# Gated mixer's core: products with the values as three products of upper and lower parts

## The chip, the cores and the metric

The kernel runs on one core of a Trainium2 chip. The time is that of one execution on the device in microseconds (us), the median of three runs of the kernel before. TensorE, VectorE (DVE in rows), ScalarE (ACT), GpSimd (POOL) and SyncE (SP, which starts the transfers of the weights) each run their own list of instructions in order and meet by semaphores.

## What is computed

A decoder trunk of two layers over 512 tokens of width 1024, in float32. Each layer is a feed-forward part, a mixer, a cross attention to 256 memory tokens and a second feed-forward part. The mixer of the second layer is a gated linear attention, the only part that is touched here:

```python
def gla_mixer(h, w_in, w_g2, b_g, head_norm, w_out):
    q, k, v, g_lr, r = _split(h @ w_in, ODD_SPLITS)
    gk = jax.nn.log_sigmoid((g_lr @ w_g2 + b_g).astype(jnp.float32)) / GLA_TAU
    ...
    q_dec = q * jnp.exp(G)
    k_inv = k * jnp.exp(-G)
    k_rem = k * jnp.exp(G_last - G)
    att = jnp.where(tril, jnp.einsum('bnhid,bnhjd->bnhij', q_dec, k_inv), 0.0)
    o_intra = jnp.einsum('bnhij,bnhjv->bnhiv', att, v)

    def step(state, xs):
        qd, kr, vv, dec = xs
        o = jnp.einsum('bhid,bhdv->bhiv', qd, state)
        state = dec[..., None] * state + jnp.einsum('bhjd,bhjv->bhdv', kr, vv)
        return state, o
    ...
    o = rmsnorm(o, head_norm).reshape(Bb, S, GLA_DV).astype(h.dtype) * jax.nn.silu(r)
    return o @ w_out
```

It has 4 heads of 128 query and key and 256 value columns, and chunks of 64 tokens.

## The kernel before

The program is one function, `trunk`, with a list of work for each engine, written out by hand in order; `parts` lists the eight parts, and the gated mixer is part 5, with a function `gla` on every engine. Weights come as units of 512 KB. SyncE loads a unit into `w_raw`, ScalarE rounds it to its upper part (`split_hi`, L412), and VectorE subtracts that from the unit, which leaves the lower part (`split_lo`, L417). `split_units(i, seg, n, off)` does this for `n` units, four units ahead of the one that TensorE reads. Large products are then made of three products of the type float32r: upper by upper, and the two mixed ones (`three`, L479 to L481; `values`, L2178 to L2180). A product of two plain float32 tiles is one matmul call, which the trace shows as two loads of the stationary operand (PEld) and two MATMUL records.

In `gla` the projections run in the order q, k, v, r, out. The values v of 4 x 128 tokens by 1024 columns are made in two halves, in the banks 4 to 7 and then 0 to 3 of PSUM, and ScalarE copies each half to `g_v` with one instruction over four banks (L1236 and L1239, semaphore `v_ready`). TensorE then transposes `g_kr` (k_rem) in four times four blocks (L2526, banks 4 to 7), ScalarE copies them to `g_krt` (L1243), and TensorE projects seven of the eight units of r (`project`, L479 to L481, banks 0 and 1), which ScalarE copies through Silu (L970) with a split behind each copy. Before its loop ScalarE loads the table for Sqrt (L1247).

The core is a loop over sixteen steps w, four heads n for each of four tiles T of 128 tokens. TensorE does in step w:

- scores (L2560): `g_k` by `g_q`, 128x128, plain float32, into a bank that two steps share; waits for the mask of step w-2
- states (L2566): for the two chunks a of the tile, 64 rows of `g_krt` by 64 rows of `g_v`, 128x256, each into a bank of its own; the two use the upper and lower 64 rows of the array; waits for S of step w-2
- `mixed(w - 1)`: scores times values (L2543, `g_att` by `g_v`, 128x256), which waits for the mask and for both states of step w-1; then the query times the state (L2549, 64 output rows for each chunk) on top of it in the same bank

VectorE does in step w: the mask (L1922, PSUM to `g_att`), then the states of the two chunks (L1931 a copy, where there is none before, L1933 otherwise; in the last tile only one). In step 0 it also splits one unit (L417). Behind steps 7, 11 and 15 it takes the norm of a tile that is done (`mean` L1954 and L1955, `normed` L1963 and four times L1966). ScalarE copies `mixed` to `f` (L1251) and squares it (L1254, semaphore `osq`), and every fourth step takes a root (L1258). `w_free`, `p_free`, `att_full`, `att`, `S`, `o_full` are semaphores.

## Time and profile before

| | us |
|---|---|
| median of 3 runs | 2206.42 (2205.71 to 2206.72) |
| the profiled execution | 2203.32 |
| its span on the core | 2201.6 |
| TensorE busy in the span | 2181.0 |
| VectorE busy | 1458.9 |
| ScalarE busy | 1125.9 |

The profiled execution is one of its own; its time is 3.1 us under the median. The span is the stretch from the first to the last instruction. A busy TensorE counts the records of its matmuls, whose ends are modelled: consecutive records overlap, so what a group of matmuls costs is read from the chain, where each piece ends as the next begins.

### The profile page before, as it was taken

How to read it: one execution, taken by the hardware profiler on the slowest of the kernel's cores; microseconds unless marked ns; L12 is line 12 of the kernel's file. 1: busy time of each engine (PE TensorE's matmuls, PEld its weight loads, DVE VectorE, ACT ScalarE, POOL GpSimd, SP SyncE). 2: the span in 40 equal slices, each digit the busy share in tenths (PEclk: the TensorE clock that was granted, in tenths of full speed). 3: DMA queues.
4: the chain of work that ended last, by engine and by line, in shares of the span. 5: the costliest groups of instructions: out<-in, count | busy, mean ns of one | idle time of the engine just before them, and what ended most of it. 6: DMA issues, size and time to landing. Idle time of an engine off the chain costs nothing.

```text
span 2201.6 us, 36639 instructions
## 1 busy us (share of the span) xinstructions
PE 2181.0 (99%) x13844; PEld 1943.8 (88%) x13844; DVE 1458.9 (66%) x2187; ACT 1125.9 (51%) x1881; POOL 108.6 (5%) x102
## 2 busy tenths in 40 slices
PE   9999999999999999999999999999999999999999
PEld 8999888765888899998899998887858888999987
DVE  7888535797666598874388885345266666888732
ACT  6555534467554555563265554245345546555531
POOL 0000000575000000000000000000000000000000
PEclk9999999999999999999999999999999999999999
DMA  4333332221352233333323333322304422333332
GB/s 162 107 104 96 115 104 74 77 86 39 125 172 67 77 115 105 105 109 101 115 87 105 103 97 115 108 88 82 100 27 145 154 77 77 105 105 105 108 100 79
DMA packets 61953, 221.44 MB, mean 101 GB/s; under 512 B 7953, under 2 KB 8081, under 8 KB 61858
## 3 DMA queue, kind: packets, MB, share of 16 engines
q1 hardware_dynamic: 57456, 208.69, 29.0%
q10 hardware_dynamic: 4402, 11.46, 1.5%
q8 instruction: 62, 1.02, 0.2%
q14 instruction: 33, 0.27, 0.0%
HBM read 218.03 MB, written 2.10 MB: 100 GB/s over the span
## 4 chain that ended last, share of the span: by engine, by line
PE 91%; DVE 6%; ACT 1%; issue 1%; DMA 0%; POOL 0%; DVEq 0%; SPq 0%; POOLq 0%; ACTq 0%
PE ps L2082 12%; PE ps L2084 12%; PE ps L2083 12%; PE ps L2178 11%; PE ps L2180 11%; PE ps L2179 11%; PE ps L479 6%; PE ps L480 5%; PE ps L481 5%; PE ps L2018 1%; DVE e_sc L1746 1%; DVE e_max L1745 1%; DVE w_lo L417 1%; DVE e_sc L1761 1%; PE ps L2566 0%
## 5 line engine op out<-in xcount | busy, mean ns | idle before, releaser
L417 DVE TENSOR_TENSOR w_lo<-w_raw,w_hi 128x1024 fp32r<-128x1024 f32 x206 | 256.7, 1249 | 362.2 <-ACT w_hi L412 361.3
L412 ACT ACTIVATE w_hi<-w_raw 128x1024 fp32r<-128x1024 f32 x210 | 221.6, 1057 | 319.7 <-PE ps L2180 224.5
L2082 PE MATMUL ps<-t_hi,w_hi 128*128 128x256 f32 x1280 | 362.3, 283 | 1.1 <-ACT tmp L843 1.1
L2083 PE MATMUL ps<-t_lo,w_hi 128*128 128x256 f32 x1280 | 362.2, 283 | 0.0
L2084 PE MATMUL ps<-t_hi,w_lo 128*128 128x256 f32 x1280 | 362.2, 283 | 0.0
L2082 PE MATMUL ps<-x_hi,w_hi 128*128 128x256 f32 x960 | 271.7, 283 | 0.0
L2083 PE MATMUL ps<-x_lo,w_hi 128*128 128x256 f32 x960 | 271.7, 283 | 0.0
L2084 PE MATMUL ps<-x_hi,w_lo 128*128 128x256 f32 x960 | 271.7, 283 | 0.0
L1475 DVE TENSOR_TENSOR w_lo<-f,w_hi 128x1024 fp32r<-128x1024 f32 x152 | 186.2, 1225 | 123.0 <-ACT w_hi L830 123.0
L479 PE MATMUL ps<-x_hi,w_hi 128*128 128x256 f32 (+1 forms) x736 | 250.9, 341 | 0.5 <-ACT g_v L1239 0.2
L2082 PEld LDWEIGHTS ps<-t_hi,w_hi 128*128 128x128 f32 x1280 | 245.7, 192 | 1.3 <-ACT tmp L843 1.3
L480 PE MATMUL ps<-x_lo,w_hi 128*128 128x256 f32 (+1 forms) x736 | 246.0, 334 | 0.0
L2084 PEld LDWEIGHTS ps<-t_hi,w_lo 128*128 128x128 f32 x1280 | 245.8, 192 | 0.0
L2083 PEld LDWEIGHTS ps<-t_lo,w_hi 128*128 128x128 f32 x1280 | 245.7, 192 | 0.0
L481 PE MATMUL ps<-x_hi,w_lo 128*128 128x256 f32 (+1 forms) x736 | 245.7, 334 | 0.0
L2178 PE MATMUL ps<-w_hi,act_hi 128*128 128x512 f32 x608 | 236.6, 389 | 0.0
L2179 PE MATMUL ps<-w_lo,act_hi 128*128 128x512 f32 x608 | 236.6, 389 | 0.0
L2180 PE MATMUL ps<-w_hi,act_lo 128*128 128x512 f32 x608 | 236.5, 389 | 0.0
L843 ACT ACTIVATE tmp<-ps 128x256 f32<-128x256 f32 x320 | 123.1, 385 | 173.9 <-PE ps L2084 171.1
L830 ACT ACTIVATE w_hi<-f 128x1024 fp32r<-128x1024 f32 x152 | 160.4, 1055 | 86.2 <-PE ps L2084 84.1
L2082 PEld LDWEIGHTS ps<-x_hi,w_hi 128*128 128x128 f32 x960 | 184.3, 192 | 0.0
L2083 PEld LDWEIGHTS ps<-x_lo,w_hi 128*128 128x128 f32 x960 | 184.3, 192 | 0.0
(350 smaller groups left out, 4311.9 us busy)
## 6 DMA issues: line engine op xcount, KB each, us to landing
w_raw<-in_wstream SPq DMA_DIRECT2D x310, 512.0 KB, 3.3
w_raw_odd<-in_wstream SPq DMA_DIRECT2D x80, 512.0 KB, 3.4
tmp<-in_post_gains ACTq DMA_DIRECT2D x8, 512.0 KB, 4.9
gain_bc<-in_gains ACTq DMA_DIRECT2D x7, 512.0 KB, 3.8
h<-in_x SPq DMA_DIRECT2D x4, 512.0 KB, 6.0
c_mem<-in_mem ACTq DMA_DIRECT2D x2, 1024.0 KB, 4.9
out_dram<-h SPq DMA_DIRECT2D x3, 512.0 KB, 2.7
c_gain<-in_mem_gains ACTq DMA_DIRECT2D x2, 512.0 KB, 6.4
```

What stands on the lines that cost most here:

```text
L412: nc.scalar.activation(weights(v)[0], raw(v), ACT.Copy).then_inc(w_hi_ready, 1)
L417: nc.vector.tensor_tensor(wl, raw(v), wh.bitcast(f32), ALU.subtract).then_inc(w_ready, 1)
L479: nc.tensor.matmul(dst, wh, xh, start=start, stop=False)
L480: nc.tensor.matmul(dst, wh, xl, start=False, stop=False)
L481: return nc.tensor.matmul(dst, wl, xh, start=False, stop=stop)
L1475: nc.vector.tensor_tensor(wl, S[:, n * UW:(n + 1) * UW], wh.bitcast(f32), ALU.subtract)\
L2082: nc.tensor.matmul(dst, wh[:, at], xh[:, b, :], start=first, stop=False, skip_group_check=True)
L2083: nc.tensor.matmul(dst, wh[:, at], xl[:, b, :], start=False, stop=False, skip_group_check=True)
L2084: last = nc.tensor.matmul(dst, wl[:, at], xh[:, b, :], start=False, stop=final, skip_group_check=True)
L2178: nc.tensor.matmul(dst, ah, wh, start=start, stop=False)
L2179: nc.tensor.matmul(dst, ah, wl, start=False, stop=False)
L2180: return nc.tensor.matmul(dst, al, wh, start=False, stop=stop)
```

## The change

`g_v`, `g_krt` and `g_att` are each replaced by an upper and a lower part of type float32r, and the state products and the scores times values are made of three products. ScalarE writes the upper parts and VectorE the lower ones:

- v: ScalarE copies two banks at a time (`g_v_hi`, four instructions in place of two), and VectorE subtracts for each pair (`v_lower`, four instructions). `v_ready` counts 1 behind the first half's two pairs, and 2 and 3 behind the pairs of the second half. TensorE starts the projection of r at 2, and the core at 3.
- krt: ScalarE copies as before, into `g_krt_hi`, and VectorE subtracts (four instructions). `g_krt` now has the order head, tile.
- scores: ScalarE copies the masked scores (`att_upper`), for step w+1 ahead of its work on step w, and for step 0 ahead of the loop; VectorE subtracts behind the states of the step, and `mixed` waits for that (`att_ready`).
- `g_v_lo` lies where `f` lies, `g_krt_lo` where `g_kr` lies. The scores and the query times the state stay plain float32.

```diff
@@ -87,6 +87,8 @@
         with ExitStack() as early:
             c_v_lo = early.enter_context(nc.sbuf_tensor("c_v_lo", [P, MT, DM], f32r))
             c_p_lo = early.enter_context(nc.sbuf_tensor("c_p_lo", [P, 2, MT, SEQ], f32r))
+        with ExitStack() as early:
+            g_v_lo = early.enter_context(nc.sbuf_tensor("g_v_lo", [P, TT, DM], f32r))
         f = sb("f", [P, TT, DM])
 
         x_hi = sb("x_hi", [P, KT, SEQ], f32r)
@@ -173,10 +175,15 @@
                 return own.enter_context(nc.sbuf_tensor(name, shape, dt))
             g_q = part_sb("g_q", [P, GH, SEQ])
             g_k = part_sb("g_k", [P, GH, SEQ])
+            with ExitStack() as early:
+                g_krt_lo = early.enter_context(nc.sbuf_tensor("g_krt_lo", [P, GH, TT, P], f32r))
             g_kr = part_sb("g_kr", [P, GH, SEQ])
-            g_krt = part_sb("g_krt", [P, TT, GH, P])
-            g_v = part_sb("g_v", [P, TT, DM])
+            g_krt_hi = part_sb("g_krt_hi", [P, GH, TT, P], f32r)
+            g_v_hi = part_sb("g_v_hi", [P, TT, DM], f32r)
             g_r = part_sb("g_r", [P, KT, SEQ])
+            with ExitStack() as early:
+                g_att_hi = early.enter_context(nc.sbuf_tensor("g_att_hi", [P, 2, P], f32r))
+                g_att_lo = early.enter_context(nc.sbuf_tensor("g_att_lo", [P, 2, P], f32r))
             g_lr = part_sb("g_lr", [GR, SEQ])
             g_w2 = part_sb("g_w2", [GR, GH * GDK])
             g_t = part_sb("g_t", [P, 2, SEQ])
@@ -395,7 +402,7 @@
 
             return b == 2 and i > 0 and parts[i - 1][0] == "cross"
 
-        VG = {"ffn": 0, "cross": 2, "even": 1, "gla": 2}
+        VG = {"ffn": 0, "cross": 2, "even": 1, "gla": 3}
         V0 = [sum(VG[k] for k, _, _ in parts[:i]) for i in range(NP)]
 
         ATI = {"ffn": 0, "cross": XH * TT, "even": AH * TT, "gla": 0}
@@ -1233,20 +1240,31 @@
                     if n + 1 < GH:
                         gate_log(n + 1)
                 act.wait_ge(w_free, U[i, "v"] + 6)
-                nc.scalar.activation(g_v[:, :, 0:SEQ], ps[:, 4:8, :], ACT.Copy).then_inc(v_ready, 1)
+                for b in range(0, TT, 2):
+                    nc.scalar.activation(g_v_hi[:, b:b + 2, 0:SEQ], ps[:, 4 + b:6 + b, :], ACT.Copy).then_inc(gs["v_hi"], 1)
                 split_units(i, "v", 3, GH)
                 act.wait_ge(w_free, U[i, "v"] + 10)
-                nc.scalar.activation(g_v[:, :, SEQ:2 * SEQ], ps[:, 0:4, :], ACT.Copy).then_inc(v_ready, 1)
+                for b in range(0, TT, 2):
+                    nc.scalar.activation(g_v_hi[:, b:b + 2, SEQ:2 * SEQ], ps[:, b:b + 2, :], ACT.Copy)\
+                        .then_inc(gs["v_hi"], 1)
                 split_units(i, "v", 1, KT - 1)
                 for n in range(GH):
                     act.wait_ge(gs["krT"], n + 1)
-                    nc.scalar.activation(g_krt[:, :, n, :], bank(4 + n).rearrange("p (t c) -> p t c", t=TT), ACT.Copy)\
-                        .then_inc(gs["krt"], 1)
+                    nc.scalar.activation(g_krt_hi[:, n, :, :], bank(4 + n).rearrange("p (t c) -> p t c", t=TT), ACT.Copy)\
+                        .then_inc(gs["krt_hi"], 1)
                 act.preload_act_table(ACT.Silu)
                 project(i, "r", KT - 1, g_r, func=ACT.Silu)
                 act.preload_act_table(ACT.Sqrt)
+
+                def att_upper(w):
+                    act.wait_ge(gs["att"], w + 1)
+                    nc.scalar.activation(g_att_hi[:, w % 2, :], g_att[:, w % 2, :], ACT.Copy).then_inc(gs["att_hi"], 1)
+
+                att_upper(0)
                 for w in range(TT * GH):
                     T, n = w // GH, w % GH
+                    if w + 1 < TT * GH:
+                        att_upper(w + 1)
                     act.wait_ge(gs["o_full"], w + 1)
                     nc.scalar.activation(f[:, T, n * GDV:(n + 1) * GDV], bank(4 + w % 2)[:, 0:GDV], ACT.Copy)
                     if w > 0:
@@ -1909,7 +1927,22 @@
                     nc.vector.tensor_tensor(g_k[:, n, :], g_k[:, n, :], g_t[:, 1, :], ALU.mult).then_inc(gs["qk"], 1)
                     if n + 1 < GH:
                         gate_sums(n + 1)
-                split_units(i, "v", GH, GH)
+                def v_lower(n):
+                    b, at = 2 * (n % 2), slice(n // 2 * SEQ, (n // 2 + 1) * SEQ)
+                    dve.wait_ge(gs["v_hi"], n + 1)
+                    return nc.vector.tensor_tensor(g_v_lo[:, b:b + 2, at], ps[:, 4 - 4 * (n // 2) + b:6 - 4 * (n // 2) + b, :],
+                                                   g_v_hi[:, b:b + 2, at].bitcast(f32), ALU.subtract)
+
+                v_lower(0)
+                v_lower(1).then_inc(v_ready, 1)
+                split_units(i, "v", 3, GH)
+                v_lower(2).then_inc(v_ready, 1)
+                v_lower(3).then_inc(v_ready, 1)
+                split_units(i, "v", 1, KT - 1)
+                for n in range(GH):
+                    dve.wait_ge(gs["krt_hi"], n + 1)
+                    nc.vector.tensor_tensor(g_krt_lo[:, n, :, :], bank(4 + n).rearrange("p (t c) -> p t c", t=TT),
+                                            g_krt_hi[:, n, :, :].bitcast(f32), ALU.subtract).then_inc(gs["krt"], 1)
                 project(i, "r", KT - 2)
                 dve.wait_ge(gs["qk"], 3 * GH)
                 dve.wait_ge(gs["zero"], 1)
@@ -1933,6 +1966,9 @@
                             ins = nc.vector.scalar_tensor_tensor(new, g_S[:, n, c % 3, :], g_dec[:, n, c:c + 1], up,
                                                                  ALU.mult, ALU.add)
                         link(ins) if a == 0 and c != SEQ // CH - 2 else ins.then_inc(gs["S"], 1)
+                    dve.wait_ge(gs["att_hi"], w + 1)
+                    nc.vector.tensor_tensor(g_att_lo[:, w % 2, :], g_att[:, w % 2, :], g_att_hi[:, w % 2, :].bitcast(f32),
+                                            ALU.subtract).then_inc(gs["att_ready"], 1)
                     if w == 0:
                         split_units(i, "r", 1, KT - 2)
                     if w % GH == GH - 1 and T > 0:
@@ -2529,19 +2565,22 @@
                 pe.wait_ge(v_ready, V0[i] + 2)
                 project(i, "r", KT - 1, x_hi, x_lo)
                 pe.wait_ge(gs["krt"], GH)
+                pe.wait_ge(v_ready, V0[i] + 3)
                 pe.wait_ge(p_free, PT0[i, "r"] + KT)
                 pe.wait_ge(gs["qk"], 3 * GH)
 
                 def mixed(w):
 
                     T, n = w // GH, w % GH
-                    pe.wait_ge(gs["att"], w + 1)
+                    pe.wait_ge(gs["att_ready"], w + 1)
                     pe.wait_ge(gs["S"], w + 1)
                     if w >= 2:
                         pe.wait_ge(gs["osq"], w - 1)
                     dst = bank(4 + w % 2)
-                    nc.tensor.matmul(dst[:, 0:GDV], g_att[:, w % 2, :], g_v[:, T, n * GDV:(n + 1) * GDV],
-                                     start=True, stop=False, skip_group_check=True)
+                    heads = slice(n * GDV, (n + 1) * GDV)
+                    for k, (a, v) in enumerate(((g_att_hi, g_v_hi), (g_att_hi, g_v_lo), (g_att_lo, g_v_hi))):
+                        nc.tensor.matmul(dst[:, 0:GDV], a[:, w % 2, :], v[:, T, heads], start=k == 0, stop=False,
+                                         skip_group_check=True)
                     for a in range(2):
                         c = 2 * T + a
                         if c == 0:
@@ -2561,10 +2600,11 @@
                                          start=True, stop=True).then_inc(gs["att_full"], 1)
                         if w >= 2:
                             pe.wait_ge(gs["S"], w - 1)
-                        for a in range(2):
-                            rows = slice(a * CH, (a + 1) * CH)
-                            last = nc.tensor.matmul(bank(2 + 4 * a + w % 2)[:, 0:GDV], g_krt[rows, T, n, :],
-                                                    g_v[rows, T, n * GDV:(n + 1) * GDV], start=True, stop=True)
+                        for m, (k, v) in enumerate(((g_krt_hi, g_v_hi), (g_krt_hi, g_v_lo), (g_krt_lo, g_v_hi))):
+                            for a in range(2):
+                                rows = slice(a * CH, (a + 1) * CH)
+                                last = nc.tensor.matmul(bank(2 + 4 * a + w % 2)[:, 0:GDV], k[rows, n, T, :],
+                                                        v[rows, T, n * GDV:(n + 1) * GDV], start=m == 0, stop=m == 2)
                         last.then_inc(gs["u_full"], 1)
                     if w >= 1:
                         mixed(w - 1)
```

TensorE, the first two steps of the core, before:

```order
L2560 MATMUL ps<-g_q,g_k 128x128
L2566 MATMUL ps<-g_v,g_krt 128x256 x2
L2560 MATMUL ps<-g_q,g_k 128x128
L2566 MATMUL ps<-g_v,g_krt 128x256 x2
L2543 MATMUL ps<-g_v,g_att 128x256
L2549 MATMUL ps<-g_S,g_q 64x256
```

And now:

```order
L2599 MATMUL ps<-g_q,g_k 128x128
L2606 MATMUL ps<-g_v_hi,g_krt_hi 128x256 x2
L2606 MATMUL ps<-g_v_lo,g_krt_hi 128x256 x2
L2606 MATMUL ps<-g_v_hi,g_krt_lo 128x256 x2
L2599 MATMUL ps<-g_q,g_k 128x128
L2606 MATMUL ps<-g_v_hi,g_krt_hi 128x256 x2
L2606 MATMUL ps<-g_v_lo,g_krt_hi 128x256 x2
L2606 MATMUL ps<-g_v_hi,g_krt_lo 128x256 x2
L2582 MATMUL ps<-g_v_hi,g_att_hi 128x256
L2582 MATMUL ps<-g_v_lo,g_att_hi 128x256
L2582 MATMUL ps<-g_v_hi,g_att_lo 128x256
L2588 MATMUL ps<-g_S,g_q 64x256
```

The groups stand in the same order; a state group is now three pairs of matmuls, and scores times values three matmuls. L2549 is now L2588.

VectorE, from the last unit splits before the core to the mask of step 1, before:

```order
L417 TENSOR_TENSOR w_lo<-w_raw,w_hi 128x1024 x10
L1922 COPY_PREDICATED g_att<-g_mask,ps 128x128
L1931 COPY g_S<-ps 128x256
L1933 SCALAR_TENSOR_TENSOR g_S<-g_S,g_dec,ps 128x256
L417 TENSOR_TENSOR w_lo<-w_raw,w_hi 128x1024
L1922 COPY_PREDICATED g_att<-g_mask,ps 128x128
```

And now:

```order
L1933 TENSOR_TENSOR g_v_lo<-ps,g_v_hi 128x2x512 x2
L424 TENSOR_TENSOR w_lo<-w_raw,w_hi 128x1024 x3
L1933 TENSOR_TENSOR g_v_lo<-ps,g_v_hi 128x2x512 x2
L424 TENSOR_TENSOR w_lo<-w_raw,w_hi 128x1024
L1944 TENSOR_TENSOR g_krt_lo<-ps,g_krt_hi 128x512 x4
L424 TENSOR_TENSOR w_lo<-w_raw,w_hi 128x1024 x6
L1955 COPY_PREDICATED g_att<-g_mask,ps 128x128
L1964 COPY g_S<-ps 128x256
L1966 SCALAR_TENSOR_TENSOR g_S<-g_S,g_dec,ps 128x256
L1970 TENSOR_TENSOR g_att_lo<-g_att,g_att_hi 128x128
L424 TENSOR_TENSOR w_lo<-w_raw,w_hi 128x1024
L1955 COPY_PREDICATED g_att<-g_mask,ps 128x128
```

The ten splits now have the lower parts of v and krt among them, and the lower part of the scores stands between the states and the unit split of step 0.

ScalarE, from the last split before the core into step 1, now; before, L1251 and L1254 (now L1269 and L1272) came right behind the table load:

```order
L419 ACTIVATE w_hi<-w_raw 128x1024
L1257 ACT_TABLE_LOAD
L1261 ACTIVATE g_att_hi<-g_att 128x128 x2
L1269 ACTIVATE f<-ps 128x256
L1272 ACTIVATE tmp,g_st<-ps 128x256
L1261 ACTIVATE g_att_hi<-g_att 128x128
L1269 ACTIVATE f<-ps 128x256
```

The upper part of the scores of steps 0 and 1 stands between the table load and the first copy.

## Rows read from the trace of the kernel before

**Rows 1.** The page: shares of the chain that ended last, by engine.

```profile
PE 91%; DVE 6%; ACT 1%; issue 1%; DMA 0%; POOL 0%; DVEq 0%; SPq 0%; POOLq 0%; ACTq 0%
```

**Rows 2.** Window: length, PE, PEld, DVE, ACT, POOL busy (x instructions); PEclk, DMA share, GB/s.

```profile
1556.00:1594.80 38.80, 38.58 (x173) 31.77 (x171) 8.59 (x7) 13.96 (x19) 0.00 (x0) 1.00 0.29 92
1594.80:1631.00 36.20, 36.12 (x186) 17.36 (x184) 24.37 (x66) 14.96 (x51) 0.00 (x0) 1.00 0.06 19
```

**Rows 3.** The chain around the core: start us, us, engine and line.

```profile
1594.93 0.22 PE ps L2560 x2
...
1609.46 0.42 PE ps L2560 x2
1609.88 0.63 PE ps L2566 x4
1610.51 0.63 PE ps L2543 x2
1611.14 0.58 PE ps L2549 x4
...
1631.03 0.43 PE ps L479
```

**Rows 4.** Timeline of TensorE in a feed-forward part: start us, us, engine, line.

```profile
2000.05 0.28 PE L2083 MATMUL ps<-t_lo,w_hi 128*128 128x256 f32 x1
2000.17 0.28 PE L2084 MATMUL ps<-t_hi,w_lo 128*128 128x256 f32 x1
```

**Rows 5.** Timeline at the end of the values: start us, us, engine, line.

```profile
1554.62 1.88 ACT L1239 ACTIVATE g_v<-ps 128x2048 f32<-128x2048 f32 x1 [4.32 <-PE ps L2180]
...
1556.56 0.50 PE L479 MATMUL ps<-x_hi,w_hi 128*128 128x512 f32 x1 [0.22 <-ACT g_v L1239]
```

**Rows 6.** Groups by line and form: count | busy us, mean ns | idle us before.

```profile
L830 ACT ACTIVATE w_hi<-f 128x1024 fp32r<-128x1024 f32 x152 | 160.4, 1055 | 86.2 <-PE ps L2084 84.1 <-DVE f L1456 2.1
...
L834 ACT ACTIVATE w_hi<-w_raw 128x512 fp32r<-128x512 f32 x40 | 24.6, 616 | 0.0
...
L986 ACT ACTIVATE c_v_hi<-ps 128x1024 fp32r<-128x1024 f32 x4 | 4.1, 1013 | 2.9 <-PE ps L2180 2.9
...
L1700 DVE TENSOR_TENSOR c_p_lo<-ps,c_p_hi 128x256 fp32r<-128x256 f32 x32 | 12.0, 417 | 8.6 <-ACT c_p_hi L1026 8.6
...
L1645 DVE TENSOR_TENSOR c_v_lo<-ps,c_v_hi 128x1024 fp32r<-128x1024 f32 x4 | 4.9, 1218 | 0.0
```

**Rows 7.** Timeline of steps 0 and 1 of the core.

```profile
1595.08 0.30 PEld L2566 LDWEIGHTS ps<-g_v,g_krt 64*128 64x128 f32 x4
...
1596.29 0.48 DVE L1933 SCALAR_TENSOR_TENSOR g_S<-g_S,g_dec,ps 128x256 f32<-128x256 f32 x1
1596.53 1.28 ACT L1247 ACT_TABLE_LOAD   x1
1596.69 1.22 DVE L417 TENSOR_TENSOR w_lo<-w_raw,w_hi 128x1024 fp32r<-128x1024 f32 x1
1596.89 0.30 PEld L2543 LDWEIGHTS ps<-g_v,g_att 128*128 128x128 f32 x2 [0.46 <-issue]
...
1599.14 0.19 PEld L2543 LDWEIGHTS ps<-g_v,g_att 128*128 128x128 f32 x1 [0.33 <-issue]
```

**Rows 8.** Timelines of VectorE behind step 7, and of VectorE and loads, steps 8 and 12.

```profile
1610.56 1.00 DVE L1933 SCALAR_TENSOR_TENSOR g_S<-g_S,g_dec,ps 128x256 f32<-128x256 f32 x2 [0.34 <-PE ps L2566]
...
1612.08 1.67 DVE L1966 SCALAR_TENSOR_TENSOR f<-f,g_st,g_gain 128x256 f32<-128x256 f32 x4
...
1613.86 0.99 DVE L1933 SCALAR_TENSOR_TENSOR g_S<-g_S,g_dec,ps 128x256 f32<-128x256 f32 x2
...
1614.96 0.30 PEld L2543 LDWEIGHTS ps<-g_v,g_att 128*128 128x128 f32 x2 [0.33 <-issue]
...
1622.91 0.47 DVE L1933 SCALAR_TENSOR_TENSOR g_S<-g_S,g_dec,ps 128x256 f32<-128x256 f32 x1
...
1624.01 0.30 PEld L2543 LDWEIGHTS ps<-g_v,g_att 128*128 128x128 f32 x2 [0.33 <-DVE g_att L1922]
```

More of the change, by code:

```diff
@@ L265, in trunk @@
         e = {n: sem("e_" + n) for n in e_names}
-        g_names = ["z_full", "z", "abs", "exp", "ln", "G", "e", "qk", "krT", "krt", "att_full", "att", "u_full",
+        g_names = ["z_full", "z", "abs", "exp", "ln", "G", "e", "qk", "krT", "krt_hi", "krt", "v_hi", "att_full", "att", "att_hi", "att_ready", "u_full",
                    "S", "o_full", "osq", "root", "on", "oT", "y", "y_hi", "y_ready", "w2_in", "gain_in",
```

## The prediction

> **What bounds the kernel now.** I read the chain of waits by engine first: TensorE holds 91% of the span [rows 1], and its clock is granted in full in both stretches that matter [rows 2], so only TensorE's time, or a wait put in front of it, moves the end. The change touches one stage, the gated mixer of part 5. In the busy time by window its core, from 1594.8 to 1631.0 us, has TensorE busy for 36.12 of 36.20 us, with VectorE at 24.37 and ScalarE at 14.96 us [rows 2]. So the core is 1.6% of the span and TensorE is its bound, but VectorE stands at two thirds of it.
>
> The chain inside the core shows what a step costs [rows 3]: scores (L2560) 0.42, the two state products (L2566) 0.63, scores times values (L2543) 0.63, state times query (L2549) 0.58, in all 2.26 us, sixteen times. The 128-column group takes 0.42 and the 256-column group 0.63, so 128 columns of plain float32 cost 0.21, 256 cost 0.43, and about 0.20 is paid per group whatever its width. The very first scores group shows the same from the other side: it follows matmuls of its own shape and takes only 0.22. The 0.20 is therefore the weight load that isn't hidden plus the change of shape (128x128, 64x128, 128x64 by turns), and it stays: no group goes away, and no shape changes. A group of the split kind pays it too: the first L479 behind a 64-column group takes 0.43 [rows 3], and 512 columns alone are worth some 0.23, twice the 0.12 of 256 [rows 4].
>
> The Trainium skill, TensorEngine Tiling (Array Packing), Key Properties, says that switching the tiling mode drains the engine; by that rule the 0.20 would stay as well, and the trace agrees with its 0.42 against 0.22.
>
> **What TensorE gains.** In 16 state groups and 16 value groups plain float32 becomes three split products. Split products of 256 columns with a new stationary operand each follow one another every 0.12 us [rows 4]. Three of them, the last without the gap behind it, are 0.12 + 0.12 + 0.107 = 0.35 where 0.43 stood. So a group falls from 0.63 to 0.55 and saves 0.08; 32 groups save 2.6 us. If the gaps vanished (0.107 each) it would be 0.107 per group, 3.4 us.
>
> For the state groups this assumes that the two 64-row halves still run side by side. The trace of before shows it for plain float32: four records take 0.63, as the two of L2543 do [rows 3]. It shows no split product of 64 rows. Side by side the group is 0.55; strictly one after the other it is 0.20 + 6 x 0.12 - 0.01 = 0.91, so 0.28 more than before. I take side by side, since the same two halves of the same array are used with the same loads, and keep 0.91 for the range.
>
> The Trainium skill, FP8 and Floating Point Precision, TensorE Precision Notes, counts four passes for true float32. By passes alone three for four would save 0.107 per group and 3.4 us in all; the pitch in the rows, 0.12 and not 0.107, says 2.6.
>
> **What is added in front of the core.** The values of banks 0 to 3 used to be freed by one copy on ScalarE (1.88 us from 1554.62), and TensorE, which had waited 0.22 us for it, went on at 1556.56 [rows 5]. Now L1248 copies two banks and VectorE subtracts, and the projection of r waits for the first such pair. The same two steps exist in the cross attention: 1.01 us on ScalarE and 1.22 on VectorE [rows 6]. So 1554.62 + 1.01 + 0.03 + 1.22 = 1556.88, plus 0.11 from VectorE to TensorE (the state ends at 1596.77, the load starts at 1596.89 [rows 7]) = 1557.00: **0.44 us lost**. The other pair of banks and the four krt lower parts (0.68 each by the slope between L1700 and L1645 [rows 6]) come while r is projected, from 1557 to 1594; only splits of later units stand behind them on VectorE, which is busy for 8.59 of 38.80 us there [rows 2]. The first half's lower parts (two of 1.22) come under the second half's products and push one unit's split by 1.5 us; TensorE reads that unit behind 1556, so they cost nothing. Uncovered, they would cost 2.4 us.
>
> **What is added in the core.** Each step gets an upper part on ScalarE and a lower one on VectorE, 128x128. Neither is in the trace. For VectorE, 256 columns take 0.417 and 1024 take 1.218, 0.134 per 128, so 128 take about 0.28 and delay the next instruction by 0.20 (a record on VectorE that waits for nothing starts 0.08 before the end of the one ahead, as L417 does behind L1933 [rows 7]). For ScalarE, 512 take 0.616 and 1024 take 1.055, a slope that gives 0.29 for 128 [rows 6]. Bounds: 0.30 from above, and 0.2 from below, half of what 256 columns take on VectorE. The product with the values now waits for the lower part.
>
> *Step 0.* ScalarE runs in order: the copy of r, a split, then the Sqrt table load at 1596.53, 1.28 us long [rows 7]. Before, nobody waited for it; ScalarE's first work in the loop came at 1598.2. Now the first upper part stands behind it: 1597.81 + 0.29 = 1598.10, lower part to 1598.42, TensorE at 1598.53 against 1596.89. **1.64 us late.**
>
> *Step 1.* VectorE stood waiting for that upper part. Its unit split (1.22, next start 1.13 later), which ran from 1596.69, now starts at 1598.33. Then L1922 at 1599.47, the state copy 1599.67, the second state 1600.12, the lower part 1600.52 to 1600.80, TensorE at 1600.91 against 1599.14: **1.77 us late**, which has swallowed what the first groups save.
>
> From there TensorE is the bound again. In an ordinary step VectorE needs 0.20 + 0.51 + 0.40 + 0.20 = 1.3 of 2.10 us, and the lower part is ready some 0.7 us before it is asked for. Left to save: 15 value groups and 13 state groups at 0.08, **2.24 us**.
>
> *Step 8.* Behind step 7 VectorE takes the norm of the first tile: states of 7 from 1610.56, the norm behind it to 1613.7, the mask of 8, and the states of 8 until 1614.85, without a gap. TensorE's group of step 8 starts at 1614.96, 0.11 later: there is no slack at all [rows 8]. The chain grows by 0.20 (lower part of 7) and 0.20 (lower part of 8, which ends 0.20 behind the state). TensorE's path between the same points has four changed groups and shrinks by 0.32. It waits **0.72 us**.
>
> *Step 12.* The same, but only one state is updated, and the slack was 0.52 (1622.91 + 0.47 + 0.11 against 1624.01 [rows 8]): 0.40 + 0.32 - 0.52 = 0.20, and 0.08 because ScalarE's upper part now ends behind that one state: **0.28 us**. Behind step 15 only the last group follows, with 0.2 to spare.
>
> Sum for the core: 1.77 - 2.24 + 0.72 + 0.28 = +0.53. With 0.44 ahead of it: **+1.0 us**. Against the profiled execution (2203.32 us) that is 2204.3; its own median runs 3.1 higher, so I put it on the median: 2206.42 + 1.0 = **2207.4 us**. The bounds of the small terms (0.107 or 0.12 per product, 0.2 or 0.3 for the two parts) move this by -1.0 to +0.4.
>
> **The rivals.**
>
> *A. The 64-row halves run one after the other.* State groups of 0.91 in place of 0.63. Fourteen of them behind step 0 cost 3.9, sixteen value groups give 1.3 back, step 0 costs 1.64, and the waits of steps 1, 8 and 12 vanish in the longer period: +4.3, with 0.44 +4.7, **2211.1 us**, on the other side of +0.2%. It passes 0.2% only where a pair takes nearly the double of one product's 0.12. Against it: four records in 0.63 [rows 3].
>
> *B. In the 64-row groups a stationary operand isn't loaded under the running product.* Then each of three rounds is load plus product, 0.21, and the group takes 0.74, 0.11 more than before: +2.3 in the core, **2209.2 us**. Against it: the first state group's four loads all lie within 0.30 us of its start [rows 7] and the group takes 0.63, so the second pair of loads ran under the first pair of products. The Trainium skill, TensorE: Matmul & The Clock Gate, Part 3, "What overlaps and what doesn't", says that a load overlaps a running matmul only where the row group differs; by it this rival would hold, and the full array's pitch of 0.12 speaks against it.
>
> *C. A clear gain.* If split groups didn't pay the 0.20 between groups, TensorE would save 0.28 in each of 32, but VectorE's chains (steps 0, 1, 8, 12) would remain, and by the same sum the core would end 3.5 us earlier: with 0.44, **2203.3 us**, still within 0.2%. Against it: the L479 of 0.43 [rows 3].
>
> *D. Step 0 doesn't wait* (the upper part gets ahead of the table load): then -1.0 in the core, **2205.9 us**. Against it: ScalarE runs in order.
>
> **How the numbers follow.** Runs of before lie within 1 us, and about 0.2% (4.4 us) is what a measurement of this kernel tells from no change. Forecast 0.74 (own range 2206.0 to 2208.4), A 0.11, B 0.06, C 0.03, D 0.06. Below 2202.0 lies only the far tail of C: 0.02. Above 2210.8 lies most of A and something unseen: 0.09. Same: 0.89. The range reaches down to D with its small terms (-1.0) and the spread of the runs, 2204.6, and up to the upper bound of the pair, 2211.1.
>
> **What would show it.** Right: L2606 and L2582 at 0.55 a group; an idle of TensorE of some 1.9 us before the first L2582 with ScalarE's table load ahead of it; 0.7 us before step 8 and 0.3 before step 12; the first projection of r at 1557.0; the core at 36.7 us. Wrong: L2606 at 0.9 or 0.74 (A, B); a lower part of over 0.4 us; waits in every step, which would mean that VectorE or ScalarE has become the bound throughout; or a difference outside the mixer, of which this sum knows nothing.

## The result, and the profile after

The changed kernel takes **2223.74 us** (median of 11 executions, 2207.33 to 2231.07) against 2205.65 us of the kernel before (11 executions beside it, 2203.79 to 2206.72): a ratio of 1.0075, 95% interval 1.0054 to 1.0097. The forecast was 2207.4 us with 2211.1 as the upper end. The profiled execution of after took 2223.74 us, its span is 2222.0 us, 20.4 more than before.

The page of after, shares of the chain by engine, for [rows 1]:

```profile
PE 89%; DVE 7%; ACT 2%; DMA 1%; issue 1%; POOL 0%; DVEq 0%; SPq 0%; POOLq 0%; ACTq 0%
```

Nothing in it tells of a new bound. The busy time by window does, for [rows 2]: projection of r, first steps of the core, the rest of the core but four steps, and what follows (length, busy us of PE, PEld, DVE, ACT, POOL, then **PEclk**, the granted clock, DMA share, GB/s):

```profile
1556.00:1595.20 39.20, 38.58 (x178) 31.94 (x177) 12.24 (x13) 15.39 (x20) 0.00 (x0) 1.00 0.29 94
1595.20:1603.80 8.60, 6.76 (x39) 5.04 (x38) 3.98 (x8) 3.23 (x5) 0.00 (x0) 1.00 0.19 63
1603.80:1641.40 37.60, 37.60 (x152) 22.94 (x151) 19.51 (x58) 11.99 (x46) 0.00 (x0) 0.50 0.04 15
1641.40:1660.00 18.60, 18.21 (x117) 13.16 (x115) 11.75 (x33) 10.37 (x28) 0.00 (x0) 1.00 0.00 1
```

For 37.6 us, nearly three quarters of the core, TensorE is granted half its clock, 1.2 GHz in place of 2.4. Before, the same place reads 1.00 [rows 2]. The chain of waits shows what stands in front of the fall, for [rows 3] (start us, us, engine and line; L2599 scores, L2606 states, L2582 scores times values, L2588 query times state):

```profile
1599.34 1.05 ACT w_hi L419
1600.40 1.28 ACT L1257
1601.69 0.32 ACT g_att_hi L1261
1602.04 0.30 DVE g_att_lo L1970
1602.38 0.62 PE ps L2582 x3
...
1604.04 0.94 PE ps L2606 x5
1604.98 0.94 PE ps L2582 x3
1605.91 1.05 PE ps L2588 x2
1606.96 0.73 PE ps L2599 x2
...
1640.55 0.94 PE ps L2606 x5
1641.49 0.55 PE ps L2582 x3
1642.04 0.58 PE ps L2588 x4
1642.62 0.42 PE ps L2599 x2
1643.04 0.55 PE ps L2606 x6
...
1650.07 0.43 PE ps L486
```

The first four pieces are the predicted wait of step 0: a split, the Sqrt table load, the upper part, the lower part. The timeline of TensorE (start us, us, instruction, in brackets the idle before it) gives its size, and the sizes of the new groups before the clock fell:

```profile
1598.64 0.38 PE L2599 MATMUL ps<-g_q,g_k 128*128 128x128 f32 x2
1598.95 0.39 PE L2606 MATMUL ps<-g_v_hi,g_krt_hi 64*128 64x256 f32 x2
...
1599.50 0.49 PE L2599 MATMUL ps<-g_q,g_k 128*128 128x128 f32 x2
...
1602.38 0.39 PE L2582 MATMUL ps<-g_v_hi,g_att_hi 128*128 128x256 f32 x1 [1.84 <-DVE g_att_lo L1970]
```

The first state group takes 1599.50 - 1598.95 = 0.55 us, as forecast. TensorE then stands for 1.84 us, as forecast. From 1603.8 a step takes 0.73 + 0.94 + 0.94 + 1.05 = 3.66 us; from 1641.49 it takes 0.42 + 0.55 + 0.55 + 0.58 = 2.10. So 37.6 us at the lower level hold about 10.3 steps, each 1.56 us too long: **16.0 us**.

The core, from the first L2599 to the first L486 behind it, takes 1650.07 - 1598.64 = 51.43 us; before it was 1631.03 - 1594.77 = 36.26 (the first L2560 has its first MATMUL record at 1594.77). That is 15.2 of the 20.4 us. Of the rest, 3.4 lie ahead of the values, 0.4 between values and projection of r, and 1.4 behind the core, where TensorE waits 0.7 and 0.4 us at projections that had no such wait in the profile of before. The kernel with one filler product (below), which has the same code there, has no such waits either, so they belong to this execution and not to the change.

The 3.4 us ahead lie in the even mixer, whose code the change doesn't touch. A window there, after and then before (a second one of 3.4 us, from 518.4, has 0.50 in after too):

```profile
487.70:494.50 6.80, 6.47 (x17) 4.55 (x18) 5.40 (x17) 2.56 (x10) 6.46 (x7) 0.50 0.38 139
```

```profile
487.70:494.50 6.80, 5.58 (x27) 4.04 (x28) 6.63 (x23) 3.47 (x14) 6.55 (x6) 1.00 0.46 154
```

And yet TensorE's idle in front of it is the same in both kernels, 3.13 us in after and 3.17 in before:

```profile
488.03 1.23 PE L2469 MATMUL ps<-e_kT,e_qT 64*128 64x256 f32 x4 [3.13 <-DVE e_st L1868]
```

```profile
488.92 0.70 PE L2433 MATMUL ps<-e_kT,e_qT 64*128 64x256 f32 x4 [3.17 <-DVE e_st L1850]
```

So the profiled execution of before happened to keep its clock there, and that is what sets its 2203.32 us apart from its median. The profiled executions of all ten experiments, where this part is unchanged, have a lower stretch near 488 us, and eight of them a second one near 517; in the kernel with one filler product they put the core's start 2.6 us later, beside the 0.4 for the values. Each execution comes with its mean clock: those of before run from 2202.61 us at 1.000 to 2206.80 us at 0.998 over all comparisons (one of 6836.98 us, in a slow state, is left out). Those of after run from 2207.33 us at 0.998 over 2218.41 at 0.992 to 2231.07 at 0.985. The one execution of after with a clock like that of before is at 2207.33, the forecast's 2207.4. The other ten lie 2.8 to 23.7 us above it. At a loss of 1.56 in 3.66 us, and if all of it fell in the core, that would be 7 to 56 us at the lower level, an estimate: the length differs from execution to execution, from a fraction of the core to the whole of it.

### The profile page after: what moved, and what is told of

The parts are those of the page before. It is cut to its first block, busy times and chain, and to the rows that moved or that the text cites. A ratio compares the mean times of both kernels' runs of the same rounds, so it can differ in the third digit from the quotient of the medians.

```text
span 2222.0 us, 36778 instructions
## 1 busy us (share of the span) xinstructions
PE 2197.6 (99%) x13892; PEld 1958.6 (88%) x13892; DVE 1469.1 (66%) x2211; ACT 1130.7 (51%) x1899; POOL 108.2 (5%) x102
## 3 DMA queue, kind: packets, MB, share of 16 engines
q8 instruction: 63, 1.03, 0.2%
## 4 chain that ended last, share of the span: by engine, by line
PE 89%; DVE 7%; ACT 2%; DMA 1%; issue 1%; POOL 0%; DVEq 0%; SPq 0%; POOLq 0%; ACTq 0%
PE ps L2118 12%; PE ps L2120 12%; PE ps L2119 12%; PE ps L2214 11%; PE ps L2215 11%; PE ps L2216 11%; PE ps L486 5%; PE ps L487 5%; PE ps L488 5%; DVE e_sc L1764 1%; DMA w_raw<-in_wstream 1%; DVE e_max L1763 1%; DVE w_lo L424 1%; PE ps L2054 1%; PE ps L2588 1%
## 5 line engine op out<-in xcount | busy, mean ns | idle before, releaser
L486 PE MATMUL ps<-x_hi,w_hi 128*128 128x256 f32 (+1 forms) x736 | 252.4, 343 | 2.6 <-DVE x_lo L1370 1.3
```

The costliest lines, as they stand in the source:

```text
L486: nc.tensor.matmul(dst, wh, xh, start=start, stop=False)
```

## The experiments

Theory: the 1.84 us idle of step 0 makes the clock fall, and behind it the changed core gets it back late. Rivals: the lighter mix of the core would lower the clock without any idle; or the new waits and instructions cost more than their sum says. Letters in the expectations name theories within that expectation.

### The upper part of step 0 ahead of the last split and the table load

```diff
-                project(i, "r", KT - 1, g_r, func=ACT.Silu)
+                project(i, "r", KT - 1, g_r, func=ACT.Silu, before_last=lambda: att_upper(0))
                 act.preload_act_table(ACT.Sqrt)
...
-                att_upper(0)
```

`project` calls `before_last` behind its last copy and ahead of the last `split_hi`.

> The changed kernel with one edit: ScalarE takes the upper part of step 0's scores ahead of its last unit split and of the Sqrt table load, so TensorE's idle of 1.9 us before the first value group shrinks to about 0.4 us. Theory I (the idle lowers the clock, and the clock lowered for the whole core is the loss): full clock in the core in nearly all runs, 2205 to 2208 us. Theory P (split products occupy the array less than plain ones and lose the clock by themselves, wait or no wait): half clock for some 37 us in most runs, 2215 to 2230 us as in the changed kernel.

Measured: **2205.37 us** (11 executions, 2202.18 to 2206.06, clocks 0.998 and 0.999) against 2205.36 of before: 1.0000, 0.9991 to 1.0010. Window over the core, and TensorE's waits of steps 0 and 1 in its timeline:

```profile
1596.00:1631.30 35.30, 33.93 (x235) 21.20 (x233) 27.15 (x81) 19.34 (x67) 0.00 (x0) 1.00 0.06 20
```

```profile
1598.24 0.39 PE L2582 MATMUL ps<-g_v_hi,g_att_hi 128*128 128x256 f32 x1 [0.27 <-DVE g_att_lo L1970]
...
1600.74 0.39 PE L2582 MATMUL ps<-g_v_hi,g_att_hi 128*128 128x256 f32 x1 [0.34 <-DVE g_att_lo L1970]
```

All work of the change is in this kernel, only one small instruction stands elsewhere, and 18 us are gone. The lighter mix alone didn't lower the clock in any of the eleven, and the added work doesn't cost what was lost. The core takes 1631.30 - 1596.07 = 35.23 us, 1.03 less than before: the forecast's case D, which had -1.0.

### The upper part between the split and the table load

```diff
-                act.preload_act_table(ACT.Sqrt)
                 def att_upper(w):
                     ...
                 att_upper(0)
+                act.preload_act_table(ACT.Sqrt)
```

> The changed kernel with step 0's upper part between ScalarE's last split and the Sqrt table load: an idle of 0.6 to 0.7 us before the first value group, where the changed kernel has 1.9 and the kernel with the upper part ahead of the split 0.45. If the length of this one idle decides, full clock and 2205 to 2206.5 us; if any idle ahead of the split core puts it at risk, some runs at half clock, over 2210 us.

Measured: 2205.76 us (11 executions, 2203.74 to 2207.00) against 2205.72: 1.0000, 0.9992 to 1.0009. The timeline shows TensorE idle for 0.42 us in step 0, and the clock stays at 1.00 through the core:

```profile
1600.87 0.39 PE L2582 MATMUL ps<-g_v_hi,g_att_hi 128*128 128x256 f32 x1 [0.42 <-DVE g_att_lo L1970]
```

### The idle filled, wholly and in part

The order of all engines as in after, but TensorE does plain products into an unused bank while it waits for step 0's lower part: four of 256 columns in one kernel, one in the other.

```diff
+                    if w == 1:
+                        for k in range(4):
+                            nc.tensor.matmul(bank(5)[:, 0:GDV], g_k[:, 0, 0:P], g_q[:, 0, 0:GDV], start=True, stop=True)
                     if w >= 1:
                         mixed(w - 1)
```

> The changed kernel with one addition: before the first value group TensorE does four plain products of 256 columns into a bank that is free, about 2 us of work in place of the idle of 1.9 us; the rest of the core is the same. Theory I: full clock in the core, 2206 to 2209 us. Theory P: half clock for some 37 us in most runs, 2215 us and more.

> The changed kernel with one plain float32 product of 256 columns (0.43 to 0.49 us, not used) in the idle of step 0, where the filled one had four: TensorE's idle there is about 1.35 us in place of 1.9. Theory O (it is the idle that brings the clock down): between the 0.65 us that left the clock in full and the 1.9 us that brought it down in nearly every execution; I expect that some executions keep the clock and others lose it, a median between 2206 and 2216, and single ones at both ends. Rival S (the clock falls at this place because of the lighter work of the core, whatever the idle): a median as the change's, 2220 to 2228. If the idle decides and 1.35 us is short enough, the median is 2205.5 to 2207 and no execution is over 2209.

Measured, four products: **2206.37 us** (11 executions, 2204.06 to 2207.97) against 2205.36: 1.0007, 0.9998 to 1.0017. One product: 2206.58 us (12 executions) against 2205.22: 1.0015, 0.9997 to 1.0034. Eleven of the twelve lie between 2203.88 and 2208.62 us at clocks of 0.997 and above; **one is at 2229.90 us at 0.985**. This is the trace of the kernel with one product, from an execution at 0.998: TensorE in step 0, and in the chain the groups behind the waits of steps 1, 8 and 12 and the end of the core:

```profile
1597.76 0.38 PE L2599 MATMUL ps<-g_q,g_k 128*128 128x128 f32 x2
...
1601.50 0.39 PE L2582 MATMUL ps<-g_v_hi,g_att_hi 128*128 128x256 f32 x1 [1.21 <-DVE g_att_lo L1970]
```

```profile
1603.88 0.62 PE ps L2582 x3
...
1619.24 0.63 PE ps L2582 x3
...
1627.90 0.63 PE ps L2582 x3
...
1634.44 0.43 PE ps L486
```

The filler takes nothing away from the waiting: the lower part comes when it came in after. What is gone is TensorE's standing still, all of it or a third of it, and 17 us with it. With 1.21 us of idle one execution in twelve lost what after loses in its worst ones; that it fell at this place is read from its time and mean clock alone, since it has no trace. With 1.84 us (after) ten of eleven lost something, and with 0.42 none of eleven did. The granted clock is 1.00 from 1597.7 to 1634.4. The core of this kernel is the changed core at the full clock, and it takes 1634.44 - 1597.76 = **36.68 us**: the forecast said 36.7.

### The same idle in the kernel before

`mixed(0)` of the kernel before waits for three small copies of ScalarE behind the table load; all products stay as they were.

```diff
                 act.preload_act_table(ACT.Sqrt)
+                act.wait_ge(gs["att"], 1)
+                for k in range(3):
+                    nc.scalar.activation(tmp[:, 2, k * P:(k + 1) * P], g_att[:, 0, :], ACT.Copy).then_inc(gs["hold"], 1)
...
                     pe.wait_ge(gs["S"], w + 1)
+                    if w == 0:
+                        pe.wait_ge(gs["hold"], 3)
```

> The kernel before with one edit: the first value group also waits for three small copies that ScalarE does behind its Sqrt table load, which gives TensorE an idle of 1.5 to 1.9 us at the same place, with plain products as before. Theory I: half clock in the core in most runs, 2215 us and more. Theory P: full clock in the core and +1.5 to +2 us, 2207 to 2208 us. If an idle and weaker products are both needed, as Theory P.

Measured: 2207.33 us (11 executions, 2206.03 to 2212.97) against 2205.36: 1.0018, 1.0009 to 1.0028. TensorE's idle in step 0, one group at the lower clock in the chain, and the window at the lower clock (L2549 is its scores times values):

```profile
1601.60 0.67 PE L2549 MATMUL ps<-g_v,g_att 128*128 128x256 f32 x2 [1.84 <-ACT tmp L1250]
```

```profile
1604.52 1.15 PE ps L2549 x2
```

```profile
1603.00:1606.40 3.40, 3.40 (x10) 1.37 (x9) 1.20 (x3) 0.69 (x3) 0.00 (x0) 0.50 0.17 60
```

An idle of the same length at the same place lowers the clock here too, in the profiled execution (2209.39 us). But **it is back after 3.4 us**, where after needed 37.6. And it doesn't fall each time: the first scores times values start 3.91 us behind the core's start against 2.15, 1.76 us late, so the idle's length alone gives 2205.36 + 1.76 = 2207.1. The median and five more (2206.03 to 2207.33) are there, as theory P had it, and the other five (2209.39 to 2212.97) are above it. So the price of the idle is set by what follows it. TensorE is busy for the whole of the lower stretch in both (3.40 of 3.40, 37.60 of 37.60), so the busy time doesn't tell them apart; the kind of products does.

### Which products keep the clock down

Three kernels with the whole list of after, its copies, subtractions and the idle (1.84 us with split states; 1.68 with plain ones, whose groups are longer). The first leaves the two mixed products out of states and values and makes the product of the upper parts as a plain float32 one; the second does so in the values alone, the third in the states alone.

```diff
-                    for k, (a, v) in enumerate(((g_att_hi, g_v_hi), (g_att_hi, g_v_lo), (g_att_lo, g_v_hi))):
-                        nc.tensor.matmul(dst[:, 0:GDV], a[:, w % 2, :], v[:, T, heads], start=k == 0, stop=False,
-                                         skip_group_check=True)
+                    nc.tensor.matmul(dst[:, 0:GDV], g_att_hi[:, w % 2, :].bitcast(f32), g_v_hi[:, T, heads].bitcast(f32),
+                                     start=True, stop=False, skip_group_check=True)
```

(and the same with `g_krt_hi` for the states.)

> The changed kernel with all its copies, subtractions and waits, but the state products and the scores times values are one plain float32 product each, of the upper parts alone (the lower parts are made and left out of the products). Theory I: half clock in most runs, as in the changed kernel, 2215 us and more. Theory P: full clock in the core, 2206.4 + 0.4 + about 2 = 2208 to 2209 us.

> The changed kernel, with its idle of 1.9 us, but scores times values are one plain product of the upper parts (the lower parts are left out there); the state products stay split. Known by now: the idle lowers the clock, and behind it plain products bring it back within 4 us and split ones do not before the core ends. Theory O (it takes the mean occupation of the array over the core; one kind of group split is half way): the clock comes back inside the core, later than with plain products, 2209 to 2220 us. Theory R (the 64-row split groups are the ones that hold it down): half clock to the end of the core, 2215 to 2230 us as in the changed kernel.

> The changed kernel, with its idle of 1.9 us, but the state products are one plain product of the upper parts for each half (the lower parts are left out there); scores times values stay split. Theory O: as the kernel with plain values, the clock comes back inside the core, 2209 to 2220 us. Theory R: the clock comes back within 4 us, 2208 to 2212 us.

| products of states / values | us, executions | ratio | lower clock in the core, profiled execution | mean clocks |
|---|---|---|---|---|
| plain / plain | 2211.20 (8) | 1.0025 (1.0015 to 1.0036) | 3.4 us | 0.996 to 0.999 |
| plain / split | 2215.49 (5) | 1.0045 (1.0032 to 1.0058) | 6.8 us | 0.993 to 0.997 |
| split / plain | 2214.52 (12) | 1.0036 (1.0023 to 1.0049) | 30.7 us | 0.989 to 0.998 |
| split / split (after) | 2223.74 (11) | 1.0075 (1.0054 to 1.0097) | 37.6 us | 0.985 to 0.998 |

One window of each of the three, in the table's order:

```profile
1604.00:1607.40 3.40, 3.40 (x10) 1.30 (x8) 2.06 (x7) 1.03 (x5) 0.00 (x0) 0.50 0.46 154
```

```profile
1601.00:1607.80 6.80, 6.80 (x21) 3.50 (x20) 3.46 (x11) 2.08 (x9) 0.00 (x0) 0.50 0.20 77
```

```profile
1602.50:1633.20 30.70, 30.70 (x106) 15.90 (x106) 14.48 (x42) 9.21 (x35) 0.00 (x0) 0.50 0.05 17
```

With both kinds of group plain, the copies and subtractions of after do little harm: the clock is back after 3.4 us in the profiled execution. The median, 2211.20, lies between the two theories (2208 to 2209, and 2215 and more). With one kind of group split the clock stays down longer, and with both longest. One profiled execution of each is thin evidence for the order of the two middle rows: their medians are within 1 us of each other, and the profiled execution of plain / split is its fastest (2208.55, the others 2213.15 to 2216.74), that of split / plain one of its slowest. What holds is that both lie between the outer two: eight of twelve executions of split / plain and four of five of plain / split are slower than every one of plain / plain (2212.41 at most), and six of eleven of after are slower than every one of the other three (2222.35 at most). By the ratios' intervals alone plain / plain and split / plain are clear of after, and the other pairs overlap. The forecast that plain states alone would bring the clock back within 4 us (theory R, 2208 to 2212) fell with 2215.49. In after the clock came back at 1641.4, 8.7 us before the core's end, so "split ones do not before the core ends" in the expectation is too strong.

### Dense work put into the core

After with its idle, and five plain products of 512 columns in front of `mixed(4)`.

```diff
                     dst = bank(4 + w % 2)
+                    if w == 4:
+                        for k in range(5):
+                            nc.tensor.matmul(dst, g_k[:, 0, 0:P], g_q[:, 0, :], start=True, stop=True)
```

> The changed kernel with its idle of step 0 left as it is, and five plain float32 products of 512 columns (10 MATMUL records of 512 columns, of g_k by g_q, into the bank that step 4's product with the values overwrites) put in front of mixed(4); their result isn't used. At the full clock they cost TensorE 5 x 0.86 = 4.3 us, at the lower one 8.6 us. Theory O (behind a fall of the clock, it comes back once TensorE is given dense work, and the core's small split groups aren't that): the clock falls at about 1603, and comes back within a few us of the burst, which starts at about 1614, so the lower stretch ends by 1625 in most executions; the time is 4.3 us plus 6 to 10 us over the before, 2216 to 2220, with single executions closer together than those of the change (2207 to 2231). Rival F (the stretch has a length of its own, set by the fall, or only the end of the core ends it): the clock stays low to 1636 or beyond as in the change, the burst costs 8.6 us more, and the median is 2228 to 2235.

Measured: **2218.75 us** (5 executions: 2211.96, then 2218.70 to 2218.84) against 2205.22: 1.0054, 1.0041 to 1.0067. The burst (L2582 in this kernel) in the chain, and the windows:

```profile
1614.75 0.94 PE ps L2609 x5
1615.68 6.88 PE ps L2582 x10
...
1624.49 0.55 PE ps L2585 x3
```

```profile
1603.40:1620.50 17.10, 17.10 (x53) 9.64 (x53) 6.58 (x19) 4.68 (x18) 0.00 (x0) 0.50 0.09 31
1620.50:1636.00 15.50, 14.90 (x98) 9.04 (x96) 9.63 (x29) 6.52 (x25) 0.00 (x0) 1.00 0.01 2
```

The clock comes back at 1620.5, 4.8 us after the burst began, where after stays low until 1641.4. This kernel spends 6.88 us on products that nobody uses and is 5.0 us faster than the change by the two medians. The intervals of the two ratios overlap; the firmer sign is that four of its five executions lie within 0.14 us, where those of after are spread over 23.7. So the fall doesn't set the length of the stretch: dense work ends it soon, and the core's own work ended it only after 37.6 us. The split groups behind the burst keep the full clock (0.55), as those of after do behind 1641.4: they hold it, and are slow to regain it.

### The waits taken out as well

The first experiment with three more moves: VectorE's unit split from step 0 to step 3, the four head norms behind steps 7 and 11 spread over the steps that follow, and the second half of the values freed in pieces of one, one and two banks, so that the projection of r can start behind the first.

```diff
-                    if w == 0:
+                    if w == 3:
                         split_units(i, "r", 1, KT - 2)
                     if w % GH == GH - 1 and T > 0:
                         mean(T - 1)
-                        normed(T - 1)
+                        scaled(T - 1)
...
+                    elif T >= 2:
+                        normed_head(T - 2, n)
```

> A version meant to be better than both: the changed kernel with step 0's upper part ahead of ScalarE's last split, VectorE's unit split moved from step 0 to step 3, the four head norms that stand behind steps 7 and 11 spread one or two to a step, and the second half of the values freed bank by bank. No idle of TensorE over 0.3 us in the core. From the sum of the prediction: 32 x 0.08 = 2.6 us saved, 0.4 lost at step 0, up to 0.2 won before the projection of r: 2203.0 to 2203.6 us against 2205.4, if the clock stays full; 2206 and more if the spread work only moves the waits.

Measured: **2202.70 us** (11 executions, 2200.31 to 2204.02) against 2205.72: **0.9984**, 0.9975 to 0.9993. It is faster than both kernels, and 0.3 us under the low end of what was expected. The chain of its core has one wait, in step 0, and from there TensorE's pieces follow one another to the end (L2607 scores times values, L2613, L2624 and L2631 the others):

```profile
1599.06 0.62 PE ps L2607 x3
1599.68 0.57 PE ps L2613 x2
1600.25 0.42 PE ps L2624 x2
1600.67 0.55 PE ps L2631 x6
...
1630.80 0.43 PE ps L486
```

The core takes 1630.80 - 1596.89 = 33.9 us (the first L2624 record is at 1596.89), 2.35 less than before: nearly the 2.6 us that 32 groups of 0.08 were to give.

## Why the prediction was wrong

**What failed** is the step headed "Step 0", with the sentence that opened the argument, "its clock is granted in full in both stretches that matter". Both were true of the profile of before. The error was to carry the second over to a kernel with "an idle of TensorE of some 1.9 us before the first L2582" and to cost that idle at its own length, 1.64 us late. It came as predicted, 1.84 us of idle, and then took some 16 us more through the clock. None of the rivals had it; the slowest, A, ended at 2211.1. The last part of the prediction even named the idle as what would show it right.

The trace of before gave no warning by itself: TensorE idles 3.17 us in the even mixer there and keeps its clock. The warning was that the median "runs 3.1 higher" than the profiled execution, which was used as an offset and not asked for its cause. The cause is the clock: the profiled execution was at 1.000 and the median ones at 0.998. A kernel whose executions differ by their clock is one where a new idle can cost more than its length.

**The other terms, at the full clock.** The kernel with one filler product has the waits of after unchanged and its clock in full, so its core can be held against the sum:

| step of the prediction | forecast | measured |
|---|---|---|
| "What TensorE gains": a group | 0.63 to 0.55 | 0.55, both kinds |
| "What is added in front of the core" | 0.44 | 1560.39 - 1558.05 = 2.34 against 1.94 [rows 5]: 0.40 |
| "Step 0", first value group late | 1.64 | 1601.50 - 1597.76 = 3.74 against 2.15: 1.59 |
| "Step 1", late | 1.77 | 1603.88 - 1597.76 = 6.12 against 4.38: 1.74 |
| "Step 8" | 0.72 | 0.66 |
| "Step 12" | 0.28 | 0.26 |
| the core | 36.7 (+0.53) | 36.68 (+0.42) |
| case D, no wait in step 0 | -1.0 | -1.03 |

2.15 and 4.38 are from the first L2560 to the first L2543 of the same two steps in the trace of before:

```profile
1594.77 0.38 PE L2560 MATMUL ps<-g_q,g_k 128*128 128x128 f32 x2
...
1596.92 0.67 PE L2543 MATMUL ps<-g_v,g_att 128*128 128x256 f32 x2
...
1599.15 0.70 PE L2543 MATMUL ps<-g_v,g_att 128*128 128x256 f32 x2
```

Against steps of 2.10 us the starts of L2582 in the filled kernel's chain, 1601.50, 1603.88, seven steps on 1619.24, and four on 1627.90, are late by 0.28, 0.66 and 0.26. The values' copy and subtraction, for the 0.40, and the start of r in the chain of after:

```profile
1558.05 1.03 ACT g_v_hi L1248
1559.11 1.24 DVE g_v_lo L1933
...
1560.39 0.50 PE ps L486
```

By the sum the kernel with the idle filled would be 1.0 us over before; it measured 1.0 with four products (2206.37 against 2205.36) and 1.4 with one. The same table closes the account of after: 16.0 us for the clock, less the waits of steps 1, 8 and 12, which the longer period swallows (0.28 + 0.66 + 0.26 = 1.2), make 14.8 over 36.68, or 51.5 us; the core took 51.43.

**Rivals.** A (0.91) and B (0.74) fell: the state group is 0.55 with 64-row halves and loads under running products. The Trainium skill, TensorE: Matmul & The Clock Gate, Part 3, "What overlaps and what doesn't", by which B would have held, is not borne out by this group. C fell: every split group still pays its 0.20. D was right as an if: the first experiment is that kernel.

**What was shown and what was argued.** Shown: without the idle, or with it filled, the loss is gone; with the same idle and plain products it is small; with dense work in the core it ends early. That the chip made the difference is ruled out: the experiments ran on three chips, and on each of them a kernel with the long idle had the lower clock in its core beside one without the long idle that kept it. Shown by counts alone, and so thinly: that 1.21 us of idle is a risk, and that 1.84 lowers the clock in most executions in front of split groups (ten of eleven) and in about half in front of plain ones (five of eleven, by their times). Not settled: what in the split groups keeps the clock from coming back. Their type, their number of products and their length all differ from the plain ones, and no run changed one of them alone. Nor is it known what brought it back at 1641.4 in after, amid the same groups.

## What to carry to other kernels

When a change puts a new idle in front of TensorE, don't cost it at its length alone: ask what runs right behind it. Dense products got the clock back within 3.4 us here, a stretch of small split products was at half clock for 37.6. If the idle can't be moved away, fill it; unused products in it cost nothing and saved 17 us. And when a profiled execution and the median differ by more than the executions scatter, look at the mean clock of each before using the difference as an offset.

## What the runs showed of the hardware that I had not expected

- An idle of TensorE of 1.84 us, behind some 40 us of unbroken work, was followed by the granted clock going to its lower level (at 1603.8, 1.4 us after work had resumed at 1602.38). It did so in most executions, not in all: ten of eleven in front of split groups, five of eleven in front of plain ones. At 1.21 us it seems to have happened in one execution of twelve, at 0.42 in none of eleven.
- At the lower level a group isn't twice as long: 0.42 to 0.73, 0.55 to 0.94, 0.58 to 1.05. A group of split products at 1.2 GHz (0.94) is still shorter than the plain one at 1.2 GHz (1.15 in the kernel before with the added wait).
- The lower level went on for 37.6 us in which TensorE was busy for 37.60. The Trainium skill, TensorE: Matmul & The Clock Gate, Part 1, "What's actually happening", describes the lower level as the default that activity releases; this trace agrees for plain products (3.40 us) and shows that a TensorE that the profile calls busy may still not be released.
- The same idle doesn't do the same in each execution: before's 3.17 us in the even mixer left its profiled execution at the full clock, and after's 3.13 brought 6.8 us at the lower one.
